# Two dense attentions of one kernel, cut by head pairs and query tiles instead of by heads

## What is computed

```
k_all = concatenate([kc, kx]);  v_all = concatenate([vc, vx])     # 256 context + 256 latent keys
def attend(q, k, v):
    s = einsum('bqhgd,bkhd->bhgqk', q, k) * scale
    p = softmax_f32(s)
    return einsum('bhgqk,bkhd->bqhgd', p, v)
out_x = attend(qx, k_all, v_all) @ w_out     # latent queries see all 512 keys
out_c = attend(qc, kc, vc) @ w_out           # context queries see the 256 context keys
```

## Time and profile before

| | us |
|---|---|
| median of 3 runs | 2516.79 |
| lowest, highest | 2514.39, 2521.75 |
| the profiled execution, its time | 2518.76 |
| the same execution, its span | 2517.0 |

### The profile page before, as it was taken

How to read it: one execution, slowest core, us unless ns; L and a number is a source line. 1 busy time by engine, 2 the same in 40 slices (tenths; PEclk the granted TensorE clock), 3 DMA queues, 4 the chain that set the end, 5 groups by cost and what they waited for, 6 DMA issues and landing times.

```text
span 2517.0 us, 31931 instructions
## 1 busy us (share of the span) xinstructions
PE 2235.8 (89%) x12968; PEld 1876.8 (75%) x12968; DVE 1413.9 (56%) x2188; ACT 1064.2 (42%) x1684; POOL 456.5 (18%) x345
## 2 busy tenths in 40 slices
PE   5988798899999898899977788999978899989997
PEld 3754476787878754799976778999975877777775
DVE  1325526855644446577467444444455477777775
ACT  2334423322334324466454135444143466666664
POOL 0300003100100310122021231111000033333332
PEclk8988998988999899999988888999776899999998
DMA  6320043444422220145632002554340377777773
GB/s 281 115 87 17 17 151 117 168 164 145 176 101 84 72 84 34 68 168 180 211 112 90 1 34 94 184 190 162 118 167 4 113 289 295 272 271 283 283 274 129
DMA packets 53193, 365.19 MB, mean 145 GB/s; under 512 B 5936, under 2 KB 8752, under 8 KB 9392
## 3 DMA queue, kind: packets, MB, share of 16 engines
q1 hardware_dynamic: 49488, 357.06, 38.6%
q10 hardware_dynamic: 3552, 6.01, 0.7%
HBM read 362.00 MB, written 1.05 MB: 144 GB/s over the span
## 4 chain that ended last, share of the span: by engine, by line
PE 72%; DVE 10%; ACT 8%; POOL 5%; issue 4%; DMA 1%; ACTq 0%; DVEq 0%; POOLq 0%; SPq 0%
PE ps L74 20%; PE ps L77 17%; PE ps L78 16%; PE ps L79 16%; POOL WLO L91 3%; ACT R L85 3%; ACT WHI L85 3%; PE ps L82 2%; DVE SM L105 2%; DVE R L91 2%; DVE R L88 1%; DVE WLO L91 1%; DVE R L95 1%; POOL h L95 1%; DMA SC<-cc 1%
## 5 line engine op out<-in xcount | busy, mean ns | idle before, releaser
L91 DVE TENSOR_TENSOR WLO<-ring,WHI 128x1024 fp32r<-128x1024 f32 x492 | 669.1, 1383 | 255.6 <-ACT WHI L85 255.0
L85 ACT ACTIVATE WHI<-ring 128x1024 fp32r<-128x1024 f32 x557 | 568.1, 1052 | 136.9 <-PE ps L79 122.1
L77 PE MATMUL ps<-HHI,WHI 128*128 128x256 f32 (+1 forms) x1680 | 552.0, 329 | 34.5 <-DVE WLO L91 12.7
L78 PE MATMUL ps<-HLO,WHI 128*128 128x256 f32 (+1 forms) x1744 | 562.4, 322 | 0.0
L79 PE MATMUL ps<-HHI,WLO 128*128 128x256 f32 (+1 forms) x1680 | 543.6, 324 | 0.0
L74 PE MATMUL ps<-R 128*128 128x128 f32 (+11 forms) x2000 | 362.8, 353 | 36.8 <-DVE R L96 16.8
L77 PEld LDWEIGHTS ps<-HHI,WHI 128*128 128x128 f32 x1680 | 332.2, 198 | 73.8 <-issue 42.1
L78 PEld LDWEIGHTS ps<-HLO,WHI 128*128 128x128 f32 x1744 | 344.4, 197 | 21.1
L74 PEld LDWEIGHTS ps<-R 128*128 128x128 f32 (+4 forms) x2000 | 248.4, 186 | 142.9 <-issue 84.8
L79 PEld LDWEIGHTS ps<-HHI,WLO 128*128 128x128 f32 x1680 | 331.2, 197 | 22.3
L85 ACT ACTIVATE R<-ps 128x512 f32<-128x512 f32 (+6 forms) x252 | 124.3, 497 | 287.2 <-PE ps L74 121.2
(11 more groups left out here) (156 smaller groups left out, 3138.4 us busy)
## 6 DMA issues: line engine op xcount, KB each, us to landing
ring<-W SPq DMA_DIRECT2D x340, 1024.0 KB, 4.8
x<-xt ACTq DMA_DIRECT2D x1, 2048.0 KB, 12.9
CR<-const_rw ACTq DMA_DIRECT2D x1, 640.0 KB, 4.0
CR<-const_nsa ACTq DMA_DIRECT2D x1, 544.0 KB, 4.8
x<-sgu_rows ACTq DMA_DIRECT2D x2, 256.0 KB, 5.9
out<-x SPq DMA_DIRECT2D x1, 512.0 KB, 3.0
out<-x ACTq DMA_DIRECT2D x1, 512.0 KB, 3.0
CR<-const_gqa ACTq DMA_DIRECT2D x1, 320.0 KB, 3.8
```

The source lines that it names most:

```text
L77: self.e.matmul(out, l[0], r[0], start=start, stop=False)
L78: self.e.matmul(out, l[0], r[1], start=False, stop=False)
L85: return self.e.activation(out, in_, func, **kw)
L91: return self.e.tensor_tensor(out, in0, in1, op)
```

## The change

Work goes by items `(pair, first query tile, number of tiles, key tiles)`. GQA has three items for each pair of heads: tiles 0 and 1 together (2 x 256 columns fill a bank for each head), tile 2, tile 3. MLA has two, one for each tile. Each item takes one score bank and one transposed bank for each of its two heads. In scores and values the products of head 0 and 1 of the pair alternate. Step i of the pipeline has, on TensorE, scores i+1, transposes i-1, values i-2; on DVE maxima i, normalising i-1, copy i-2; on ScalarE exponential i, copy i-2, output i-3. The output bank of a pair is taken out of the turn while its items add to it. DVE copies the first head's bank, ScalarE the second's. The maxima of a bank are one reduction. Scores of GQA wait for their own pair's rotated queries in place of the last one's, and V is awaited at the values alone. GQA's scale factors (`RQ`) are made after the first V copy rather than after the fourth. The splitting of weights stands after items 18 (and 20 on DVE) of 24 and 10 (and 12) of 16.

```diff
-        def scores_pe(self, pe, hd):
...
+        def scores_pe(self, pe, i):
+            pr, q0, nq, nk = self.items[i]
+            bs = [take(pe, ("S", self.key, i, z), ("exp", self.key, i, z)) for z in range(2)]
+            for ev in self.ready(pr):
                 pe.wait_ge(*at(*ev))
+            for q in range(nq):
+                for z in range(2):
+                    hd, o = 2 * pr + z, 128 * nk * q
+                    t = pe.mm(bs[z][:, o:o + 128 * nk], self.q(hd, q0 + q), self.k(hd, 128 * nk), True, True)
+            t.then_inc(*did("scores", ("scores", self.key, i)))
...
+        def max_dve(self, v, i):
+            pr, q0, nq, nk = self.items[i]
+            m = mx[:, i % 2, 0:2 * nq]
+            v.wait_ge(*at("scores", self.key, i))
+            if i >= 2:
+                v.wait_ge(*at("exp", self.key, i - 2, 1))
+            for z in range(2):
+                v.rmax(m[:, nq * z:nq * z + nq], rows3(bank("S", self.key, i, z)[:, :], 128 * nk), negate=True).then_inc(
+                    *did("softmax"))
...
+        def exp_act(self, a, i):
...
+            a.wait_ge(*at("max", self.key, i))
+            if i >= 2:
+                a.wait_ge(*at("turned", self.key, i - 2))
+            for z in range(2):
+                for q in range(nq):
...
+                t.then_inc(*did("exp", ("exp", self.key, i, z)))
...
+        def turn_pe(self, pe, i):
+            pr, q0, nq, nk = self.items[i]
+            bs = [take(pe, ("T", self.key, i, z), ("pt", self.key, i, z)) for z in range(2)]
+            pe.wait_ge(*at("weights", self.key, i))
+            for z in range(2):
+                for kt in range(nk):
+                    for q in range(nq):
+                        c = 128 * (kt * nq + q)
+                        t = pe.transpose(bs[z][:, c:c + 128], self.p(i, z, q)[:, 128 * kt:128 * kt + 128], ident)
...
+        def copy(self, e, i, z):
+            e.wait_ge(*at("turned", self.key, i))
+            if i >= 2:
+                e.wait_ge(*at("pv", self.key, i - 2))
+            d, s = self.PT[:, i % 2, 512 * z:512 * z + 512], bank("T", self.key, i, z)[:, :]
+            t = e.act(d, s, ACT.Copy) if z else e.cp(d, s)
...
+        def values_pe(self, pe, i):
+            pr, q0, nq, nk = self.items[i]
+            if i % self.per == 0:
+                self.O = take(pe, ("O", self.key, pr), ("out", self.key, pr))
+                keep(bank_of["O", self.key, pr])
+            for ev in self.values:
+                pe.wait_ge(*at(*ev))
+            for z in range(2):
+                pe.wait_ge(*at("pt", self.key, i, z))
+            for kt in range(nk):
+                for z in range(2):
+                    t = pe.mm(self.O[64 * z:64 * z + 64, 128 * q0:128 * (q0 + nq)], self.v(2 * pr + z, kt),
+                              self.PT[:, i % 2, 512 * z + 128 * nq * kt:512 * z + 128 * nq * (kt + 1)], kt == 0, kt == nk - 1)
+            t.then_inc(*did("values", ("pv", self.key, i)))
+            if i % self.per == self.per - 1:
+                give(bank_of["O", self.key, pr])
...
-        "gqa", 16, [2, 2, 4, 4],
+        "gqa", 16, [2, 2, 4, 4], [(0, 2), (2, 1), (3, 1)],
...
-        [("gkd",), ("gfin", 7), ("gvt", 3)], lambda hd: RQ[:, :, hd])
+        lambda pr: [("gkd",), ("gfin", pr)], [("gvt", 3)], lambda q, hd: RQ[:, q, hd])

     def attend_pe(pe, A, step=None):
...
+        A.scores_pe(pe, 0)
+        for i in range(A.n + 2):
+            if i + 1 < A.n:
+                A.scores_pe(pe, i + 1)
+            if 1 <= i <= A.n:
+                A.turn_pe(pe, i - 1)
+            if i >= 2:
+                A.values_pe(pe, i - 2)
+            if step:
+                step(i)
...
-        "mla", 16, [4, 4],
+        "mla", 16, [4, 4], [(0, 1), (1, 1)],
```

More of the change, by code:

```diff
@@ L1290, in program @@
     class Attention:
[L1291 to L1297, removed]
@@ L1312, in score, with __init__ @@
[L1312 to L1325, removed]
+        def __init__(self, key, heads, nk, items, q_ap, k_ap, v_ap, scale, PB, PT, out, parts, ready, values, own=None):
+            self.key, self.nk, self.q, self.k, self.v = key, nk, q_ap, k_ap, v_ap
+            self.scale, self.PB, self.PT, self.out, self.parts = scale, PB, PT, out, parts
+            self.ready, self.values, self.own, self.per = ready, values, own, len(items)
+            self.items = [(pr, q0, nq, nk[q0]) for pr in range(heads // 2) for q0, nq in items]
+            self.n = len(self.items)
@@ L1331, in soften_dve @@
[L1331 to L1341, removed]
@@ L1362, in turn_copy @@
[L1362 to L1372, removed]
@@ L1374, in values_pe @@
[L1374 to L1383, removed]
@@ L1385, in values_act, with p @@
-        def values_act(self, a, hd):
-            if hd % 2 == 0:
+                m = m.rearrange("p (h q) -> p h q", q=nq)
+                t = v.tt(m, m, self.own(slice(q0, q0 + nq), slice(2 * pr, 2 * pr + 2)).rearrange("p q h -> p h q"), ALU.mult)
+            else:
+                t = v.ts(m, m, self.scale, None, ALU.mult)
+            t.then_inc(*did("softmax", ("max", self.key, i)))
+        def p(self, i, z, q):
+            n = 128 * self.items[i][3]
+            return self.PB[:, i % 2, 512 * z + n * q:512 * z + n * q + n]
@@ new lines, in copy @@
+        def copy(self, e, i, z):
[4 more added lines that the diff above has]
+            t = e.act(d, s, ACT.Copy) if z else e.cp(d, s)
+            t.then_inc(*did("turned_act" if z else "turned_dve", ("pt", self.key, i, z)))
+        def values_pe(self, pe, i):
+            pr, q0, nq, nk = self.items[i]
+            if i % self.per == 0:
[6 more added lines that the diff above has]
+            for kt in range(nk):
+                for z in range(2):
+                    t = pe.mm(self.O[64 * z:64 * z + 64, 128 * q0:128 * (q0 + nq)], self.v(2 * pr + z, kt),
[3 more added lines that the diff above has]
+                give(bank_of["O", self.key, pr])
@@ L1387, in values_act, with out_act @@
+        def out_act(self, a, i):
+            pr, last_ = i // self.per, i % self.per == self.per - 1
+            if not last_:
                 return
-            pr = hd // 2
-            a.wait_ge(*at("pv", self.key, hd))
-            a.act(self.out(pr), bank("O", self.key, pr)[:, 0:128 * self.nq], ACT.Copy).then_inc(
+            a.wait_ge(*at("pv", self.key, i))
+            a.act(self.out(pr), bank("O", self.key, pr)[:, 0:128 * len(self.nk)], ACT.Copy).then_inc(
                 *did("att_out", ("out", self.key, pr)))
@@ new lines, in attend_act @@
+    def attend_act(a, A, step=None):
+        for i in range(A.n + 3):
+            if i < A.n:
+                A.exp_act(a, i)
+            if 2 <= i < A.n + 2:
+                A.copy(a, i - 2, 1)
+            if i >= 3:
+                A.out_act(a, i - 3)
+            if step:
+                step(i)
+    def attend_dve(v, A, step=None):
+        for i in range(A.n + 2):
+            if i < A.n:
+                A.max_dve(v, i)
+            if 1 <= i <= A.n:
+                A.normalise_dve(v, i - 1)
+            if i >= 2:
+                A.copy(v, i - 2, 0)
+            if step:
+                step(i)
@@ L1599, in attend_pool @@
     def attend_pool(g, A):
-        pipeline_heads(A.heads, None, None, None, lambda hd: A.values_pool(g, hd), None)
+        for pr in range(A.n // A.per):
+            A.low_pool(g, pr)
     mK, mQ = rows3(R1[:, 0:8192], 512), rows3(R1[:, 8192:12288], 256)
```

115 lines of the change are left out of this document (33 added, 82 removed).

## The result

| | us |
|---|---|
| kernel before, median of 4 runs | 2517.18 |
| changed kernel, median of 4 runs (lowest, highest) | 2422.74 (2422.32, 2424.47) |
| ratio, with its 95% interval | 0.9624 [0.9612, 0.9637] |
| span of the changed kernel's profiled execution | 2422.7 |

The change saves 94 us; the forecast was 76. Direction and mechanism were right, the size was 18 us short.

What follows compares the result with a forecast made beforehand. GQA (162.1 us) was taken as bound by TensorE's serial work plus waits, MLA (91.0 us) by TensorE's serial work. Savings of 56.6 and 19.4, sum 76, took 2517.0 to 2441 us; range 2418 to 2475.

Steps and rivals of the forecast that it cites:

- What bounds after: Both attentions after the change: a GQA item costs DVE's 3.62 us, an MLA item TensorE's 3.76, say 3.8.
- Products side by side: TensorE scores and values: array halves overlap fully, 0.86 us paired against 1.72 serial; MLA's 96-row scores stay 1.72.
- The rival's own price: TensorE, both attentions: halves don't overlap, items of 4.6 us, 31 us more, 2472; chance of no overlap 0.14.
- MLA's item: MLA attention on TensorE: transposes 0.93, scores 1.72, values 0.86, shape changes 0.25; 3.76 us, say 3.8.
- VectorE's item in GQA: GQA on DVE: reductions, small operations, weightings, one copy and 0.2 of gaps; mean 3.62 us per item.
- Start of GQA: GQA's first items: scores of items 0 and 1 end at 162, maxima of item 2 start at 166.6 us.
- Cold start: Early GQA: TensorE idles from 163 to 166.6, its clock falls, costing 5 us; ada steps 0.5.
- Splitting and the clock behind it: Splitting the next weights mid-stage: 6.9 us plus 3 for the clock in GQA, 6.5 plus 3 in MLA.
- Fill and tails: Ends of both attentions: from last maxima to last values 7.7 us in GQA; tail 7.3 in MLA.
- Ties: Rival, both attentions: a bank or ScalarE's output delays transposes, items 4.2 and 4.3 us, 2460; chance 0.15.
- The clock: Rival: TensorE's clock stays low through both attentions, items 5.6 and 7.2 us, 2528; chance 0.03.
- no cold stretch, splitting hidden: Better-than-the-sum case, both attentions: 17 us less, 2424, down to 2418; chance 0.03 beyond the forecast's own.

Runs made afterwards that it cites:

- The run with the heads apart: Changed kernel with the two heads' value and score products parted by products of another shape on TensorE; 2471.48 us.
- The run without look-ahead: Changed kernel with scores of item i, not i+1, issued first in step i on TensorE; 2568.90 us, ratio 1.0197 to the kernel before.
- the blocks of four: Changed kernel with values in blocks, two key tiles (four instructions) of head 0, then two of head 1, in place of one and one; 2424.48 us.

## Why the prediction was right, and where it was short

*What bounds after.* Right, and shown from both sides: GQA by VectorE, MLA by TensorE.

*Products side by side.* Right. It was read off 32 small instructions with 0.062 us apiece, and it holds for 256 and 512 columns. The eight pairs of value instructions of an item, all on 128 rows, take 1.02 us with the change of shape (from 898.12 to the scores at 899.15), and the whole of side by side is worth up to 49 us. The Trainium skill ("TensorE: Matmul & The Clock Gate", The mechanism) has weight loads overlap with running products only when the row group differs. The trace contradicts it: the sixteen weight loads of these values, each 0.13 to 0.14 us long, start from 898.12 to 898.84, among the sixteen products (898.12 to 898.94) and without holding them up. That the values themselves would go unpaired by that rule was my inference; the page speaks of the loads. The rival's own price was 31 us, with items of 4.6. The run with the heads apart has 5.16 and 5.02, but two more changes of shape in each item, so it doesn't price that rival exactly.

*MLA's item.* 3.8 forecast, 3.81 measured.

*VectorE's item in GQA: the mis-sized term.* Forecast 3.62, measured 3.41: 21 items make 4.4 us. I added whole durations and 0.2 of gaps; the starts show 0.18 less than the durations of an item in place of 0.2 more. Against this went one error of the other sign: GpSimd's low part beside the weightings costs 1.0 us a pair, not 0.47.

*Start of GQA.* Maxima of item 2 at 166.4 (166.6 forecast). Cold start: from item 2 to item 8 it took 24.4 us against 20.5 at the steady pace, 4 in this profile (5.5 forecast, the ada step in it), and 1.4 to 1.9 in the profiles that had one cold stretch in place of two.

*Splitting and the clock behind it: the second mis-sized term.* Forecast 6.9 + 3 in GQA and 6.5 + 3 in MLA. Measured over the steady pace: 5.7 in GQA (items 18 to 22: 23.2 us against 17.5, counting the cold stretch at 234 to 241 us) and 3.3 in MLA, where the granted clock stayed 1.00 all through. Part of the waiting was already paid in the item's own time: after VectorE's first two low parts the next items' scores and transposes stood ready, and they came at VectorE's 2.98 in place of 3.81. I had added the splitting to full items. That is 4.2 and 6.2 us.

*Fill and tails.* 7.7 forecast and measured in GQA, 7.3 and 7.6 in MLA, where also maxima of item 2 came 0.4 earlier after the start and item 3 only 3.05 after item 2 (0.8 less).

Sum: 4.4 + 1.5 + 4.2 + 0.2 in GQA, 6.2 + 0.4 + 0.8 - 0.3 in MLA, and 2.2 between the stages where 1.0 was counted: 18.6, less 0.2 behind them. That is the 18 us.

*Ties.* 0.15 was given to them. They don't set the pace, but stand close behind it: with one of VectorE's three copies of a pair moved to ScalarE the pair stayed at 10.29. *The clock* at 0.03: right for this order. The run without look-ahead shows its place: waits of 2.7 to 2.9 us an item cost GQA 1.6 to 2.8 us an item by the clock, while waits of 2.66 in MLA cost most items nothing.

*How near the range was to failing.* Every mis-sized term but GpSimd's and the tail of MLA erred the same way, and the range held by 4.7 us. Its lower end had been set by "no cold stretch, splitting hidden"; measured, the cold start still cost 4 us and the splitting 5.7 and 3.3, and the rest came from VectorE's shorter item.

## What to carry to other kernels

Where two products leave halves of the array free, put them within a few instructions of each other, with nothing of another shape between; strict alternation isn't needed. Packing shortens an engine's work only, and here the packed kernel without scores issued an item ahead was 50 us slower than the old one: put the look-ahead in first, then pack. When a stage becomes bound by VectorE, read its pace off start-to-start distances, not off summed durations, and look for GpSimd operations beside its SBUF-to-SBUF ones.

## What the runs showed that I had not expected

- Products for a free half of the array overtake: the second head's first of eight started with the first head's fifth. Groups of two score instructions and of four value instructions of 256 columns, written in series, paired up fully (7 and 13 ns apart); in the blocks of four with 128 columns the second block's pairs were 57 ns apart.
- The granted clock was 0.50 over the busy stretches of a pipeline that waits 2.7 to 2.9 us an item, and was 1.00 over its waits, so idling cost the products that followed and GQA's item grew from about 5.9 to 7.9 us; MLA's items with nearly the same wait mostly kept 1.00.
- A GpSimd subtraction of 1.33 us holds up two VectorE weightings by 1.01 us (0.88 to 1.89), and even an operation of four columns beside it took 0.76 in place of 0.16 us, while copies and reductions out of PSUM kept their time.
